# Residual held by tokens, with 512 moving weight columns and row statistics

## What is computed

```python
for i in range(DEPTH):                       # DEPTH = 2
    h = pool_mixer(x, ...) if i % N_MIXERS == 0 else dilated_attention(x, ...)
    x = layer_norm(DEEPNORM_ALPHA * x + h, ln_mix_g[i], ln_mix_b[i])
    x = layer_norm(DEEPNORM_ALPHA * x + sqrelu_mlp(x, mlp_w_up[i], mlp_w_down[i]), ln_mlp_g[i], ln_mlp_b[i])
...
    hn = _rmsnorm(h, attn_norm_w[l])
    ...
    h = h + y @ w_out[l]                     # y: SSM and attention halves, each RMS-normed
    h = h + _conv_ffn(_rmsnorm(h, ffn_norm_w[l]), ...)
return _rmsnorm(h, final_norm_w)
```

## Time and profile before

| | us |
|---|---|
| median of 3 runs | 3681.27 (3680.45 to 3683.77) |
| span of the profiled execution | 3673.0 |
| PE busy in it | 3439.8 (94%) |
| DVE busy | 1924.2 (52%) |
| ACT busy | 1494.7 (41%) |
| HBM read | 587.74 MB, 163 GB/s with the writes |

### The profile page before, as it was taken

The page is one execution under the profiler, slowest core; times in us unless marked ns, Lnnn a source line. Parts: engine busy times, 40 slices in busy tenths (PEclk is TensorE's granted clock), DMA queues, the critical chain, the costliest instruction groups (busy, mean ns, idle before and its releaser), DMA issues.

```text
span 3673.0 us, 64862 instructions
## 1 busy us (share of the span) xinstructions
PE 3439.8 (94%) x27648; PEld 3394.9 (92%) x27648; DVE 1924.2 (52%) x1682; ACT 1494.7 (41%) x1300; POOL 301.8 (8%) x474
## 2 busy tenths in 40 slices
PE   7898999999998999978999999989789999999997
PEld 7898999999998999977999999989679999999997
DVE  7744444454454444434555555556545565655654
ACT  4334433433334434434333333344454444444442
POOL 2201222222220000000000000003200000000000
PEclk9999999999999999988999999999899999999999
DMA  6443555555553444432555555543223455555452
GB/s 236 147 161 137 187 178 174 184 183 186 176 169 117 162 161 165 163 144 98 182 181 181 182 182 182 183 172 123 108 102 138 161 184 183 183 181 182 180 181 76
DMA packets 117668, 602.10 MB, mean 164 GB/s; under 512 B 14320, under 2 KB 47152, under 8 KB 48560
## 3 DMA queue, kind: packets, MB, share of 16 engines
q1 hardware_dynamic: 94880, 585.35, 44.6%
q10 hardware_dynamic: 22672, 15.01, 1.3%
HBM read 587.74 MB, written 12.58 MB: 163 GB/s over the span
## 4 chain that ended last, share of the span: by engine, by line
PE 81%; DVE 5%; ACT 4%; POOL 4%; issue 3%; DMA 2%; ACTq 1%; POOLq 0%; SPq 0%; DVEq 0%
PE ps L1567 25%; PE ps L1569 25%; PE ps L1568 25%; PE ps L1612 2%; DMA compact<-ssm_compact 2%; POOL b_four L1533 1%; POOL b_wide L1530 1%; ACT whi L462 1%; DVE wlo L951 1%; POOL job_tmp L1526 1%; POOL c_wide L1530 1%; ACT resid L508 1%; DMA raw<-weights 1%; ACTq L549 1%; ACT y_mix L787 1%
## 5 line engine op out<-in xcount | busy, mean ns | idle before, releaser
L951 DVE TENSOR_TENSOR wlo<-raw,whi 128x2048 fp32r<-128x2048 f32 (+2 forms) x572 | 1254.8, 2198 | 1517.6 <-ACT whi L462 1516.5
L462 ACT ACTIVATE whi<-raw 128x2048 fp32r<-128x2048 f32 (+2 forms) x572 | 1044.6, 1831 | 1796.0 <-PE ps L1569 1749.7
L1567 PE MATMUL ps<-x_pair,whi 128*128 128x256 f32 x5360 | 1528.2, 285 | 76.9 <-DVE x_pair L984 44.8
L1569 PE MATMUL ps<-x_pair,wlo 128*128 128x256 f32 x5360 | 1519.5, 283 | 0.0
L1568 PE MATMUL ps<-x_pair,whi 128*128 128x256 f32 x5360 | 1516.1, 283 | 0.0
L1567 PEld LDWEIGHTS ps<-x_pair,whi 128*128 128x128 f32 x5360 | 1015.5, 189 | 81.5 <-issue 74.8
L1568 PEld LDWEIGHTS ps<-x_pair,whi 128*128 128x128 f32 x5360 | 1021.6, 191 | 0.2
L1569 PEld LDWEIGHTS ps<-x_pair,wlo 128*128 128x128 f32 x5360 | 1016.6, 190 | 0.0
L1567 PE MATMUL ps<-hid_hi,whi 128*128 128x256 f32 x2624 | 749.5, 286 | 32.6 <-DVE resid L998 25.9
L1568 PE MATMUL ps<-hid_lo,whi 128*128 128x256 f32 x2624 | 745.4, 284 | 0.0
L1569 PE MATMUL ps<-hid_hi,wlo 128*128 128x256 f32 x2624 | 744.9, 284 | 0.0
(11 more groups left out here) (326 smaller groups left out, 2603.0 us busy)
## 6 DMA issues: line engine op xcount, KB each, us to landing
raw<-weights SPq DMA_DIRECT2D x539, 1024.0 KB, 4.8
read_tab<-read_tables SPq DMA_DIRECT2D x2, 3072.0 KB, 11.3
raw<-weights SPq DMA_DIRECT2D x8, 640.0 KB, 8.7
drive_tables<-drive_out ACTq DMA_DIRECT2D x16, 256.0 KB, 5.9
read_tables<-c_wide ACTq DMA_DIRECT2D x32, 128.0 KB, 5.8
drive_tab<-drive_tables SPq DMA_DIRECT2D x4, 1024.0 KB, 8.0
resid<-x_t SPq DMA_DIRECT2D x4, 512.0 KB, 6.5
inner_out<-ssm_skip ACTq DMA_DIRECT2D x16, 128.0 KB, 2.1
```

The source lines that it names most:

```text
L462: act.activation(whi[:, s, 0:width], raw[:, s, 0:width], ACT.Copy).then_inc(hi_ready, 1)
L951: dve.tensor_tensor(wlo[:, s, 0:width], raw[:, s, 0:width], whi[:, s, 0:width].bitcast(F32), ALU.subtract).then_inc(lo_ready, 1)
L1567: pe.matmul(o, w_hi, x_hi, start=first, stop=False)
L1569: return pe.matmul(o, w_lo, x_hi, start=False, stop=last)
```

## The change

The residual is held by tokens: two tiles of 128 tokens by 2048 features. Its projections take 128x128 of the activations as the stationary operand and 512 columns of the weights as the moving one (`rows_tile`), half as many matmuls; the weights are packed for it. A projection's last group is passed over twice, first for tokens 0 to 127 (`tail_done`), then for the rest (`down_last`). DVE adds and takes statistics of each 128x512 block (`add_half`, `block_stats`), ACT takes the root (`row_sqrt`), DVE normalises, PE transposes back into tiles by features (`turn_x`), ACT applies gain and bias out of PSUM and makes the high part (`x_piece`), DVE the low part (`x_low`). The next stage starts with two output tiles in turn, piece by piece (`pair_first`). The factor alpha with the norm's gain and bias is applied to the residual afterwards (`rescale`), with gain and bias as rows that SP loads, spread to all partitions, in nine loads. mlp1's norm is computed by rows ahead of attn2's statistics. The table loads behind mlp1 wait for the end of attn2's norm. The residual comes in by an own load on ACT's queue, and the result leaves by tokens. The norms q, kv, ssm and mla stay as they are, as do up blocks, attention and scan.

```diff
-        resid = sb("resid", [P, DT, T])
+        resid = sb("resid", [P, 2, D])
...
+            load_quads(0, QUAD["mlp0"] + 2)
+            sp.wait_ge(y_lo, 4)
+            wait_used(sp, QUAD["pool_group"])
+            load_row("mix0_g")
+            load_row("mix0_b")
+            load_quads(QUAD["mlp0"] + 2, QUAD["attn"])
+            load_quads(QUAD["attn"], QUAD["attn"] + 2, ATTN_WIDTHS)
+            sp.wait_ge(tables_stored, 48 + 48 * JOBS)
+            sp.wait_ge(inner_stored, 16 + 16 * JOBS)
+            load_row("mlp0_g")
+            load_quads(QUAD["attn"] + 2, QUAD["attn"] + 8, ATTN_WIDTHS)
+            sp.wait_ge(row_used, 1)
+            load_row("mlp0_b")
+            load_quads(QUAD["attn"] + 8, QUAD["attn_out"], ATTN_WIDTHS)
+            load_quads(QUAD["attn_out"], QUAD["mlp1"] + 2)
+            wait_used(sp, QUAD["attn_out"] + 1)
+            load_row("mix1_g")
+            load_row("mix1_b")
+            load_row("mlp1_g")
+            load_row("mlp1_b")
+            load_quads(QUAD["mlp1"] + 2, QUAD["mixer"])
...
-            wait_used(sp, QUAD["mixer"] - 1)
+            sp.wait_ge(norm_lo, LO0["attn2"] + 4)
...
+            sp.wait_ge(norm_lo, LO0["ffn2"] + 4)
+            load_row("final_g")
+            load_quads(QUAD["ffn"] + 2, N_QUADS)
...
+            def x_piece(name, y, p):
+                n = 4 * TURNED[name] + p + 1
+                gain, g0, bias, b0 = GAIN[name]
+                if LO0[name] + p >= 2:
+                    act.wait_ge(norm_lo, LO0[name] + max(0, p - 1))
+                act.wait_ge(tok_turned, n)
+                for i in range(4):
+                    k = 4 * p + i
...
+                        ins = act.activation(y[:, p % 2, i, :], block_ps(p)[:, i, :], ACT.Identity, scale=fcol(gain, g0 + k),
+                                             bias=fcol(bias, b0 + k))
+                ins.then_inc(x_scaled, 1)
+                act.wait_ge(x_scaled, n)
+                act.activation(xhi[:, 4 * p:4 * p + 4, :], y[:, p % 2], ACT.Copy).then_inc(norm_hi, 1)
+            def tail(name, eps, y, q, widths=(CW,) * 4, none=False):
+                row_sqrt(name, 0, eps)
+                if none:
+                    hi1(*PLACE["none", 0], MIXER_WIDTH["none"])
+                for s in range(3):
+                    hi1(q, s, widths[s])
+                row_sqrt(name, 1, eps)
+                x_piece(name, y, 0)
+                x_piece(name, y, 1)
+                hi1(q, 3, widths[3])
+                x_piece(name, y, 2)
+                x_piece(name, y, 3)
...
+            act.dma_start(resid[:], x_rows.rearrange("(a p) c -> p a c", p=P)).then_inc(resid_landed, 16)
...
+            def add_rows(nb, bank, sem_, n):
+                r = rows_of(resid, nb)
+                return dve.tensor_tensor(r, r, ps[:, bank:bank + 2, :], ALU.add).then_inc(sem_, n)
+            def add_half(tt, nb, bank, sem_, value):
+                r = row_block(resid, tt, nb)
+                dve.tensor_tensor(r, r, ps[:, bank, :], ALU.add).then_inc(sem_, 1)
+                dve.wait_ge(sem_, value)
+                block_stats(tt, nb)
+            def block_stats(tt, nb):
+                step(dve.bn_stats(out=row_stats[:, tt, nb, :], in_=row_block(resid, tt, nb)))
...
+            def open_rstd(name, tt):
+                dve.wait_ge(tok_std, TOKEN[name, tt] + 1)
+                step(dve.reciprocal(row_rstd[:, tt:tt + 1], row_std[:, tt:tt + 1]))
+                step.settle()
+            def normalise(name, tt):
+                open_rstd(name, tt)
+                for nb in range(4):
+                    x, r = row_block(resid, tt, nb), row_rstd[:, tt:tt + 1]
+                    if GAIN[name][2] is None:
+                        ins = dve.tensor_scalar(row_block(xn, tt, nb), x, r, None, ALU.mult)
+                    else:
+                        ins = dve.tensor_scalar(x, x, row_mv[:, tt, 0:1], r, ALU.subtract, ALU.mult)
+                    ins.then_inc(tok_xc, 1)
+            def x_low(name, y, p):
+                dve.wait_ge(norm_hi, LO0[name] + p + 1)
+                a = slice(4 * p, 4 * p + 4)
+                dve.tensor_tensor(xlo[:, a, :], y[:, p % 2], xhi[:, a, :].bitcast(F32), ALU.subtract).then_inc(norm_lo, 1)
+            def tail(name, last, sem_, base, y, q, widths=(CW,) * 4, norm_at=0, lo_at=0, n_early=1, none=False):
+                rms, n = GAIN[name][2] is None, len(last)
+                for i, (nb, banks, _, done) in enumerate(last):
+                    dve.wait_ge(tail_done, done)
+                    add_half(0, nb, banks[0], sem_, base + i + 1)
+                close_stats(0, rms)
+                for i, (nb, banks, place, _) in enumerate(last):
+                    if i == norm_at:
+                        normalise(name, 0)
+                    if i == lo_at:
+                        for s in range(n_early):
+                            lo1(q, s, widths[s])
+                    wait_used(dve, *place)
+                    add_half(1, nb, banks[1], sem_, base + n + i + 1)
+                    if none and i == 0:
+                        lo1(*PLACE["none", 0], MIXER_WIDTH["none"])
+                close_stats(1, rms)
+                normalise(name, 1)
+                if n_early < 2:
+                    lo1(q, 1, widths[1])
+                x_low(name, y, 0)
+                lo1(q, 2, widths[2])
+                x_low(name, y, 1)
+                lo1(q, 3, widths[3])
+                x_low(name, y, 2)
+                x_low(name, y, 3)
...
+            def rescale_gain(name, row_name, used=None):
+                for tt in range(2):
+                    ins = dve.scalar_tensor_tensor(out=resid[:, tt, :], in0=resid[:, tt, :], scalar=ALPHA, in1=row[row_name][:],
+                                                   op0=ALU.mult, op1=ALU.mult)
...
+            for nb in range(3):
+                lo4(q + nb + 1)
+                wait_used(dve, q + nb)
+                add_block(nb, 4 + 2 * (nb % 2), down_free, 2, u + 2 * nb + 2)
+            tail("mix0", [(3, (6, 7), (q + 3, 3), TAIL["pool_out"] + 1)], down_free, u + 6, y_ln, QUAD["mlp0"], n_early=2)
+            mlp("mlp0")
+            tail("mlp0", mlp_tail("mlp0"), down_free, UNITS["mlp0"] + 120, y_ln, QUAD["attn"], ATTN_WIDTHS, 1, 2)
...
+            q, base = QUAD["mixer"], UNITS["mlp1"] + 120
+            last = mlp_tail("mlp1")
+            dve.wait_ge(rows_landed["mlp1"], 32)
+            for i, (nb, banks, _, done) in enumerate(last):
+                dve.wait_ge(tail_done, done)
+                add_half(0, nb, banks[0], down_free, base + i + 1)
+            close_stats(0, False)
+            for i, (nb, banks, place, _) in enumerate(last):
+                wait_used(dve, *place)
+                add_half(1, nb, banks[1], down_free, base + 4 + i + 1)
+                if i == 0:
+                    gain_rows_of(0)
+                if i == 1:
+                    bias_rows_of(0)
+                if i == 2:
+                    second_stats(0)
+            close_stats(1, False)
+            gain_rows_of(1)
+            normalise("attn2", 0)
+            bias_rows_of(1)
+            second_stats(1)
+            lo1(q, 0)
+            normalise("attn2", 1)
+            lo1(q, 1)
+            x_low("attn2", y_rms, 0)
+            lo1(q, 2)
+            x_low("attn2", y_rms, 1)
+            lo1(q, 3)
+            x_low("attn2", y_rms, 2)
+            x_low("attn2", y_rms, 3)
...
+            def finish_rows(tt):
+                open_rstd("final", tt)
+                for nb in range(4):
+                    dve.scalar_tensor_tensor(out=row_block(out_rows, tt, nb), in0=row_block(resid, tt, nb), scalar=row_rstd[:, tt:tt + 1],
+                                             in1=row["final_g"][:, 512 * nb:512 * nb + 512], op0=ALU.mult, op1=ALU.mult).then_inc(tok_y, 1)
...
+            def rows_tile(o, s, tt, kts, xh, xl, first, last):
+                t = slice(tt * P, tt * P + P)
+                for j, k in enumerate(kts):
+                    c = slice(j * 512, j * 512 + 512)
+                    pe.matmul(o, xh[:, k, t], whi[:, s, c], start=first and j == 0, stop=False)
+                    pe.matmul(o, xh[:, k, t], wlo[:, s, c], start=False, stop=False)
+                    ins = pe.matmul(o, xl[:, k, t], whi[:, s, c], start=False, stop=last and j == 3)
+                return ins
+            def turn_x(name, src, sem_, value, n_free):
+                for tt in range(2):
+                    for nb in range(4):
+                        pe.wait_ge(tok_xc, 8 * TURNED[name] + 4 * tt + nb + 1)
+                        if tt == 0 and nb == n_free:
+                            pe.wait_ge(sem_, value)
+                        for i in range(4):
+                            c = slice(512 * nb + i * P, 512 * nb + i * P + P)
+                            ins = pe.transpose(block_ps(nb)[:, i, tt * P:tt * P + P], src[:, tt, c], ccol("ident"))
+                        if tt == 1:
+                            ins.then_inc(tok_turned, 1)
```

(41 more changed lines are left out.)

623 lines of the change are left out of this document (351 added, 272 removed).

## The result

The changed kernel takes 3530.53 us (median of 4 runs, 3528.3 to 3532.51), the kernel before 3681.15 beside it: a ratio of 0.9595, 95% interval 0.9582 to 0.9609. It is faster by 150 us, and the forecast was 3526. The time is right, but not all of its terms are: the biggest one, the pace of a 512-column matmul, was worth about a third of what was forecast or less, and addresses that moved without anybody's intent made up for most of what was missing.

The account below looks back on a forecast made before the run. PE was taken as the bound, busy 3439.8 of 3673.0 us, with time to save in the pace of projections into the residual and in waits for norms: 3681-70-85 = 3526 us, range 3498 to 3577.

Parts of the forecast that it names:

- The pace, 217 ns: Projections into the residual: 512-column matmuls start 217 ns apart, bounds 213 and 240, worth 70 us over all stages.
- rival 1: Projections into the residual: pace 226 ns, the 13 ns excess of 256 columns kept; gain 44, 3552 us; chance 0.10.
- rival 2: Projections into the residual: no gain from columns, 240 ns a matmul, 3596 us; chance 0.03.
- The add chain: mlp1 down projection: chunk 2 waits for chunk 0's add, 5.57 us after it, so starts at 10.84, not 10.42.
- mlp0, nothing: mlp0's loop: tables, compact's load and POOL's job set the turn, so a faster down projection gains nothing; 5 us added.
- Rival 4: mlp0's chain gives way, a POOL step not held up by DVE; groups gain 1.9 us each, 3498 us; chance 0.04.
- The norms, 85 us: Stretches where PE waits for norms: statistics run along the free axis while PE still works, saving 85 us in sum.
- Hidden: Residual load at the start, residual rescaling, row loads and transposes: costed as covered by other work, the transposes half.
- output chunks inside the MLA heads: 0: Output chunks among the MLA heads gain 0, since the heads wait for softmax steps.
- Rival 3: Projections: weight loads cannot hide under 512-column matmuls, each costs 323 ns; 3948 us; chance 0.03.
- Rival 6: Projections: 512-column passes overlap and keep 120 ns, the add chain sets a group; 3298 us; chance 0.02.
- Rival 5: Norms: statistics in two passes, 1.4 us, 3537 us; with 15 us of slow clock in mlp0, 3547; chance 0.06.

Follow-up runs that it names:

- a32: The changed kernel with the SBUF region that holds x_pair, hid, heads and the rest beginning 32 bytes later; 3562.25 us.
- the last two versions: Changed kernel with all gaining edits and three small ones, 3428.99 us; the same with 512 columns again and hid, last and mla tiles 64 bytes later, 3455.20 us.
- PE alone: Computation left out, x copied to the output, rows of matmuls run with no other engine at varied addresses; fp32r with 512 columns took 226.7 to 234.5 ns.
- the last version but one (the fastest): The changed kernel with all gaining edits, including two matmuls of 256 columns for each of 512, and three small edits; 3428.99 us, ratio to before 0.9315.

## Why the prediction was right, and where it was not

**The pace, 217 ns: wrong.** The step that failed is "At 512 columns the stream is 213 ns and the load fits in it. I take 217 ns, the fp32 row". It is 233.4 in the kernel and 226.7 to 234.5 alone, past 226, which the prediction itself had named as a sign of being wrong. Hiding of the load was right; that fp32r streams like fp32 was not. The time lies halfway between rival 1's 226 ns and rival 2's 240. Rival 1 had the better neighbour, 256 columns of the same kind, and took their excess once; it is 13 ns on 256 and 20 on 512. With 233.4 in the forecast's own sums a chunk is 5.60 us, the add at 5.57 is just in time, and the terms are 9.6 + 6.4 + 1.9 + 2.6 + 1.3 + 5.4 + 2.1 - 5 = 24 us, not 70. That would have made 3572. The add chain is where the forecast saw it. In mlp1 the third chunk starts some 0.13 us late in every down group; in ffn, where DVE has the convolution as well, it is 0.43, and a group takes 22.82 us instead of 23.13:

```profile
2930.22 0.40 PE L1857 MATMUL ps<-whi,hid_lo 128*128 128x512 f32 x1
2930.78 0.50 PE L1855 MATMUL ps<-whi,hid_hi 128*128 128x512 f32 x1 [0.16 <-DVE resid L1068]
```

**What filled the gap.** Run a32 has the up blocks at 120.0 ns, as the kernel before, so these two show the change without the placement: 114 us between their profiled executions (3673.0 and 3559.0), where the sums with 233.4 and the norms' 85 give 109. Of the difference, the norms gained 9.5 more than forecast, mlp0 6.4 more, the attention heads and output 4; mlp1 and ffn gained 6 less, pool_out and the last chunks 1 less, and 8 were lost at the start and among the MLA heads. The placement then gave 31.7 more, 5.6 of it in mlp0, whose turn is an up block and the chain behind it. With the address of before (a32) the forecast's 3526 would have been 36 us off, still inside its range. The right number was partly luck: 46 us too many in one term were made good by 32 from an address and by smaller terms. The range, which took in rival 1, is what the argument had earned.

**mlp0, nothing: right**, and by its mechanism: taking the chain away gave 45 us, and taking a hole away under it gave none. The 5 us for extra spells at the lower clock were not lost: mlp0 has nine such spells of 3.4 us instead of seven, and all nine fall into down projections, which have time in hand. PE's wait for the job is 0.5 to 2.4 us from start to start, not about 3; the rest of the time in hand went into the hole before the third chunk, 2.2 to 2.7 us. Rival 4, a POOL step not held up by DVE, named the lever, though it was seen from its other side, at 63 us.

**The norms, 85 us: right.** Without the pace's share they gained 20.8, 16.7, 25.5, 12.3, 7.2 and 11.9, together 94. Each first matmul came within 0.3 us of the 8.5 forecast, and the end took 8.5 instead of 9.0; of the 9 over, some 4 are ffn2, whose block of before carried 2.5 us of the lower clock that the term counted as 0.8. Two norms in a row took 23.4 us to the first matmul (25.3 forecast), and the stall behind them was 5.12 (5.1).

**Hidden: two were not.** The residual's load and scaling were costed at nothing with the condition that they don't delay the second weight chunk. It is ACT that they delay: 3.70 us of scaling stand ahead of the second quad's high parts, and PE's wait at 64.7 grew from 6.58 to 8.94. And "output chunks inside the MLA heads: 0" missed what an add of two banks asks of DVE's order. The third of these chunks waits for an add that stands behind a low part:

```profile
2659.81 0.38 PE L2199 MATMUL ps<-k_rope,m_io 64*128 64x256 f32 x1
2662.71 0.76 PE L1855 MATMUL ps<-whi,ssm_hi 128*128 128x512 f32 x1 [2.52 <-DVE resid L1068]
```

Three of the rows of output chunks ran partly at granted clock 0.50, 427 ns a matmul, where one did before, and these heads lost 7.0 us in all. In the last two versions, with the add moved ahead, that wait is gone and 3.9 of the 7.0 are back (220.5 us in the last); the slow spell from 2632 to 2639 stands ahead of the wait and is not its doing; before, it lasted 3.4 us at that place, and why it is longer now isn't shown.

**Rivals.** Rival 2 (240 ns, 3596 us) was as near in pace as rival 1, and 65 us off in the total. Rival 3 fell: no matmul took 323 ns. Rival 6 fell too; the Trainium skill's 131 ns at 512 columns ("TensorE: Matmul & The Clock Gate", "Back-to-back issue gap") is shown by no row of the changed kernel or of PE alone, where 227 to 235 stand. Rival 5 fell: the statistics take 0.69 us.

## What to carry to other kernels

Compare the pace of instructions that a change doesn't touch before crediting it with the gain: here a small tile left SBUF, all behind it moved by 288 bytes, and 32 us came from that. Price a new shape by the nearest row of the same data type, and take its excess over the columns along, even if another type seems to have the right cost, and count how many records one instruction leaves. Where two chains end almost together, a saving on one is worth nothing until the other is cut, and the exchange of two instructions that gains 10 us behind the cut costs 63 ahead of it: try the two together before dropping either.

## What the runs showed of the hardware that was not expected

- fp32r matmuls in a row run at one of a few fixed paces for hundreds of instructions, at granted clock 1.00 throughout: 113.3 to 120.0 ns at 256 columns, 226.7 to 234.5 at 512. The moving operand's address less the stationary one's, modulo 256, orders all that were seen.
- Where that is 64 or 192, the way into the row picks between 113.3 and 117.8. Two up blocks of mlp1 that follow each other in the last version but one (the fastest), same code and same addresses:

```profile
1757.41:1779.98 22.57, 22.57 (x194) 1.00 0.52 185
1801.80:1823.57 21.77, 21.77 (x195) 1.00 0.53 193
```

- So two matmuls of 256 columns beat one of 512: 28.7 us in this kernel.
- A POOL tensor_tensor of 0.45 us takes 2.2 to 2.6 when DVE makes a low part of 128x2048 at that time, that is, until some 0.3 us after DVE is done. In the changed kernel's turn from 578 us on, DVE's adds out of PSUM (1.21 us) held up none of the steps beside them (0.41 to 0.46).
